# A new order of weight units in the odd layer, splits asked for earlier, and the norm's weights and bias applied by VectorE instead of GpSimd

## The reference

```python
h = layer_norm(x, g, b)                       # x: 256 x 1024
q, kv, gates, cq, ckv, k_rope = split_cols(h @ w_in, ODD_SPLITS)
cq, ckv = rms_norm(cq, g_q), rms_norm(ckv, g_kv)
# branch C: compressed, selected and window attention on q and kv
blocks = gelu(flat_blocks(kv_cmp + pe) @ w1) @ w2     # for keys and for values
# branch D: latent attention
q_d, k_d, v_d = cq @ w_uq, ckv @ w_uk, ckv @ w_uv     # with rotation of 32 of 96 channels
y = concat(attention_C, attention_D)
x = h * ALPHA + y @ w_out                     # then a layer norm and a conv feed-forward
```

## Time and profile before

| | |
|---|---|
| Median of 3 runs | 1433.69 us (1433.32 to 1433.8) |
| The profiled execution | 1439.07 us, of which the span of the profile is 1437.8 us |
| TensorE busy | 1322.6 us, 92% of the span |
| VectorE busy | 897.0 us, 62% |
| ScalarE busy | 590.5 us, 41% |
| GpSimd busy | 119.5 us, 8% |
| Mean granted clock of TensorE | 0.949 of full speed |

### The profile page before, as it was taken

How to read it: one execution, slowest core, us unless ns; L and a number is a source line. 1 busy time by engine, 2 the same in 40 slices (tenths; PEclk the granted TensorE clock), 3 DMA queues, 4 the chain that set the end, 5 groups by cost and what they waited for, 6 DMA issues and landing times. The chain is left out here.

```text
span 1437.8 us, 21155 instructions
## 1 busy us (share of the span) xinstructions
PE 1322.6 (92%) x8531; PEld 1204.6 (84%) x8537; DVE 897.0 (62%) x1291; ACT 590.5 (41%) x900; POOL 119.5 (8%) x152
## 2 busy tenths in 40 slices
PE   8988999999899999979987899999789898899996
PEld 5876788878589999869977799997779888799995
DVE  5957981125566777755476666666634585666666
ACT  2331111113355555543453554555411364554553
POOL 3890000003000000010000000010400000000000
PEclk9999899999999999999997999999887798999999
DMA  9434233427045556535502355565455202355561
GB/s 282 146 95 149 83 118 126 142 94 229 25 131 181 187 177 195 185 94 176 160 17 91 136 184 178 198 204 146 107 129 165 80 1 64 134 185 178 198 210 60
DMA packets 178590, 202.76 MB, mean 141 GB/s; under 512 B 21868, under 2 KB 163147, under 8 KB 178492
## 3 DMA queue, kind: packets, MB, share of 16 engines
q1 hardware_dynamic: 174939, 191.49, 42.0%
q0 software_dynamic: 3184, 9.77, 2.3%
q10 hardware_dynamic: 369, 0.13, 0.1%
HBM read 200.30 MB, written 1.08 MB: 140 GB/s over the span
## 5 line engine op out<-in xcount | busy, mean ns | idle before, releaser
L1317 DVE TENSOR_TENSOR w_parts<-raw,w_parts 128x1024 fp32r<-128x1024 f32 (+1 forms) x268 | 333.8, 1245 | 167.1 <-ACT w_parts L1306 159.6
L1306 ACT CAST w_parts<-raw 128x1024 fp32r<-128x1024 f32 (+1 forms) x268 | 279.3, 1042 | 337.6 <-PE ps L1600 103.3
L1600 PEld LDWEIGHTS ps<-hT_parts,w_parts 128*128 128x128 f32 x3024 | 366.6, 192 | 2.1
L1600 PE MATMUL ps<-hT_parts,w_parts 128*128 128x256 f32 x3024 | 367.6, 283 | 0.0
L1613 PE MATMUL ps<-w_parts,gT_parts 128*128 128x512 f32 x720 | 168.9, 390 | 0.0
L1613 PEld LDWEIGHTS ps<-w_parts,gT_parts 128*128 128x128 f32 x720 | 133.3, 188 | 26.4
L1366 PE MATMUL ps<-w_parts,hT_parts 128*128 128x256 f32 (+1 forms) x864 | 117.6, 303 | 16.7 <-DVE w_parts L1317 12.1
L1366 PEld LDWEIGHTS ps<-w_parts,hT_parts 128*128 128x128 f32 x864 | 116.2, 212 | 18.1 <-DVE w_parts L1317 12.5
L1364 PE MATMUL ps<-hT_parts,w_parts 128*128 128x256 f32 x912 | 120.8, 298 | 8.5 <-DVE w_parts L1317 4.5
L1364 PEld LDWEIGHTS ps<-hT_parts,w_parts 128*128 128x128 f32 x912 | 119.4, 207 | 10.0 <-issue 5.0
L451 PE MATMUL ps<-hT,ring 128*128 128x256 f32 x448 | 99.0, 380 | 1.0 <-DVE hT L310 1.0
(11 more groups left out here) (407 smaller groups left out, 1519.3 us busy)
## 6 DMA issues: line engine op xcount, KB each, us to landing
raw<-in_ffn_w_up SPq DMA_DIRECT2D x44, 1024.0 KB, 5.1
raw<-in_f_w_up SPq DMA_DIRECT2D x22, 1024.0 KB, 5.1
raw<-in_ffn_w_down SPq DMA_DIRECT2D x22, 1024.0 KB, 5.1
ring<-in_w_in SPq DMA_DIRECT2D x18, 1024.0 KB, 6.1
raw<-in_ev_w_in SPq DMA_DIRECT2D x15, 1024.0 KB, 5.4
raw<-in_f_w_down SPq DMA_DIRECT2D x11, 1024.0 KB, 4.9
ring<-in_x_wkv SPq DMA_DIRECT2D x8, 1024.0 KB, 5.5
ring<-in_w_out SPq DMA_DIRECT2D x4, 1024.0 KB, 5.1
```

The lines of the kernel that those rows point to most:

```text
L1306: self.done(A, A.copy(high[:, c], self.raw[:, u % RAW, c]), self.s_hi)
L1317: self.done(V, V.tensor_tensor(low[:, c], self.raw[:, u % RAW, c], high[:, c].bitcast(F32), ALU.subtract), self.s_lo)
L1600: mm = T.matmul(self.ps[:, b, m * 256:m * 256 + 256], w[:, kk, m * P:(m + 1) * P], x[:, kk, :], start=kk == 0 and q == 0, stop=kk == KD - ...
```

## The change

The list of units gets another order behind kv1. Before it is uq0, uq1, uk, uv, q0, cmp0, q1, cmp1, k0, cmp2, k1, cmp3. After it is q0, uq0, uq1, q1, uk, uv, k0, cmp0, cmp1, k1, cmp2, cmp3. TensorE follows this order. ScalarE and VectorE ask for the splits of q0, q1, k0 and k1 earlier in their queues, so ahead of some copies out of PSUM. GpSimd's `pool_affine` is gone. VectorE applies the weights and bias in eight pieces: two after the split of kv1, two after the split of k1, and four after the split of the first unit of `w_out`. GpSimd waits for these eight before it loads the next rows. No arithmetic is changed.

```diff
+        queries(0)
+        self.u_uq.append(unit(I["od_w_uq_2"][0], 0, 3, 512, False))
+        self.u_uq.append(unit(I["od_w_uq_2"][0], 512, 3, 256, False))
+        queries(1)
         self.u_uk, self.u_uv = unit(I["od_w_uk_2"][0], 0, 2, 512, False), unit(I["od_w_uv_2"][0], 0, 2, 512, False)
+        keys(0)
+        compress(0)
+        compress(1)
+        keys(1)
+        compress(2)
+        compress(3)
...
# TensorE
         ckf = self.pe_transposes(ckn, kt=2)
+        qf_ = self.pe_late(self.u_q[0], "F", self.hparts)
         self.pe_wait_drained(cqf)
         uqf = self.pe_late(self.u_uq[0], "T", cqT) + self.pe_late(self.u_uq[1], "T", cqT)
+        qf_ += self.pe_late(self.u_q[1], "F", self.hparts)
         self.pe_wait_drained(ckf)
         ukf = self.pe_late(self.u_uk, "T", ckT)
         uvf = self.pe_late(self.u_uv, "T", ckT)
+        kf_ = self.pe_late(self.u_k[0], "F", self.hparts)[0]
         T.wait_ge(*self.s_xs.at(8))
-        qf_, self.cmp_fills = [], []
-        qf_ += self.pe_late(self.u_q[0], "F", self.hparts)
+        self.cmp_fills = []
         self.pe_compress(0, 0, XS)
-        qf_ += self.pe_late(self.u_q[1], "F", self.hparts)
         self.pe_compress(0, 1, XS)
-        kf_ = self.pe_late(self.u_k[0], "F", self.hparts)[0]
+        vf_ = self.pe_late(self.u_k[1], "T", self.hparts)[0]
         self.pe_compress(1, 0, XS)
-        vf_ = self.pe_late(self.u_k[1], "T", self.hparts)[0]
         self.pe_compress(1, 1, XS)
...
# ScalarE
+        self.act_split(self.u_kv[1])
+        self.act_split(self.u_q[0])
         self.act_drain_gain(cqf, cqT, "od_q_norm_2", kt=3)
+        self.act_split(self.u_q[1])
+        self.act_split(self.u_k[0])
+        self.act_split(self.u_k[1])
         for hh in range(2):
             self.act_evac(uvf[hh], vm[:, :, hh * 256:(hh + 1) * 256])
+        self.act_split(self.u_odo[0])
+        for kv in range(2):
+            self.act_compressed(kv, hid)
...
# VectorE
+        self.dve_split(self.u_kv[1])
+        self.dve_affine(0)
+        self.dve_affine(1)
         V.wait_ge(*self.s_zero.at(2))
+        self.dve_blocks(0, kvf[0], KS, XS)
+        self.dve_split(self.u_q[0])
+        self.dve_blocks(1, kvf[1], KS, XS)
         self.dve_drain_gain(cqf, cqT, "od_q_norm_2", kt=3)
         self.dve_drain_gain(ckf, ckT, "od_kv_norm_2", kt=2)
+        self.dve_split(self.u_q[1])
+        self.dve_evac_halves(qf_[0], qT[:, :, 0:2, :])
         for hh in range(2):
             self.dve_evac(uqf[hh], uq[:, :, hh * 256:(hh + 1) * 256])
+        self.dve_split(self.u_k[0])
         self.dve_evac(uqf[2], uq[:, :, 512:768])
+        self.dve_rotate(0, uq, qf, kf)
+        self.dve_evac_halves(qf_[1], qT[:, :, 2:4, :])
         # copies of ukf, unchanged
+        self.dve_rotate(1, uq, qf, kf)
+        self.dve_split(self.u_k[1])
+        self.dve_affine(2)
+        self.dve_affine(3)
         self.dve_evac(kf_, kT)
+        self.dve_split(self.u_odo[0])
+        for i in range(4, 8):
+            self.dve_affine(i)
         self.dve_evac(vf_, vv)
...
# GpSimd
-        self.pool_affine(8)
...
+        if l == 1:
+            self.G.wait_ge(*self.s_affine_x.at(16))
```

More of the change, by code:

```diff
@@ L1227, in late_units @@
             self.u_kv.append(len(lu) - 1)
-        self.u_uq = [unit(I["od_w_uq_2"][0], 0, 3, 512, False), unit(I["od_w_uq_2"][0], 512, 3, 256, False)]
-        self.u_uk, self.u_uv = unit(I["od_w_uk_2"][0], 0, 2, 512, False), unit(I["od_w_uv_2"][0], 0, 2, 512, False)
[L1230 to L1244, removed]
+        self.u_q, self.u_k, self.u_uq, self.u_cmp = [], [], [], []
@@ new lines, in queries, with keys @@
+        def queries(i):
+            lu.append(((KD, 2, 2, 64), lambda v: [
+                (v[:, :, m, g, :], wk[:, :, g * 256 + (2 * i + m) * 64:g * 256 + (2 * i + m) * 64 + 64])
+                for m in range(2) for g in range(2)], 4, True))
+            self.u_q.append(len(lu) - 1)
+        def keys(i):
+            lu.append(((KD, 256), lambda v, c0=768 + 128 * i: [
+                (v[:, :, 128 * b:128 * b + 128], wk[:, :, c0 + 256 * b:c0 + 128 + 256 * b]) for b in range(2)], 2, True))
+            self.u_k.append(len(lu) - 1)
@@ new lines, in compress @@
+        def compress(i):
+            kv, half = divmod(i, 2)
+            w1 = I["od_cmp_w1_2"][0, kv].rearrange("(j p) n -> p j n", p=P)
+            lu.append(((8, 256), lambda v: [(v, w1[:, 8 * half:8 * half + 8, :])], 1, False))
+            self.u_cmp.append(len(lu) - 1)
+        queries(0)
+        self.u_uq.append(unit(I["od_w_uq_2"][0], 0, 3, 512, False))
+        self.u_uq.append(unit(I["od_w_uq_2"][0], 512, 3, 256, False))
+        queries(1)
+        self.u_uk, self.u_uv = unit(I["od_w_uk_2"][0], 0, 2, 512, False), unit(I["od_w_uv_2"][0], 0, 2, 512, False)
@@ L1549, in pool_rows @@
         self.G.dma_start(self.rowsb[:, i, 0:n], src.partition_broadcast(P)).then_inc(*self.s_rows[i].inc(16))
[L1551 to L1559, removed]
     def new_ffn(self, l, at):
@@ L2373, in layer_tail @@
         self.new_stats(2)
-        self.G.wait_ge(*self.s_affine_x.at(8 * l + 8))
+        self.G.wait_ge(*self.s_affine_x.at(16 * l + 8))
         for i in range(2):
@@ L2523, in odd_layer @@
             self.drain(V, V.tensor_copy(part(1), src(1)), f)
[L2524 to L2530, removed]
+        self.dve_rotate(1, uq, qf, kf)
+        self.dve_split(self.u_k[1])
+        self.dve_affine(2)
+        self.dve_affine(3)
         self.dve_evac(kf_, kT)
-        self.dve_split(self.u_cmp[2] + 1)
-        self.dve_split(self.u_k[1] + 1)
+        self.dve_split(self.u_odo[0])
+        for i in range(4, 8):
+            self.dve_affine(i)
         self.dve_evac(vf_, vv)
-        self.dve_split(self.u_cmp[3] + 1)
         V.wait_ge(*self.full(kcf))
@@ L2543, in odd_layer @@
         self.dve_parts(yf)
-        V.wait_ge(*self.s_affine.at(2))
         for c, u in enumerate(self.u_odo):
```

21 lines of the change are left out of this document (1 added, 20 removed).

## The result

The changed kernel takes 1421.16 us (median of 4, 1419.36 to 1422.45), where the kernel before takes 1433.74 (1433.32 to 1439.42). The ratio is 0.9889, with a 95% interval of 0.9863 to 0.9916. The medians differ by 12.6 us, and I had forecast 8.0.

The account below looks back on a forecast made before the run. TensorE, busy in 92% of the span, was taken to bound the kernel through its waits and clock. Moving cmp3's end from 1120.7 to 1112.8 gave 8.0 us off the 1433.7 median: 1425.7 us, range 1418.5 to 1431.

Parts of the forecast that it names:

- half clock of 2.5 us: In uv's second half and k0: TensorE's clock falls after uv's waits, costing 2.5 us.
- part 1: At od1 and od2: without GpSimd's four operations VectorE's split halves speed up, and od2 ends 6.8 us earlier.
- rival D: At od1 and od2: GpSimd and VectorE do not disturb each other, leaving 1.2 us gained, 1432.5 us; chance 0.07.
- parts 2 and 3: kv1 still waits, nothing gained; q0 fills the wait of 3.07 us before uq0, with VectorE's two pieces hidden behind kv1.
- q1's split in time: At q1: its weights are split at 1051.2, before TensorE needs them at 1057.0, so it runs at full clock.
- parts 5 and 6: From uv through k0: waits of 2.3 and 3.6 us at uv, then 2.5 us of half clock; k0 ends at 1084.1.
- part 6: Compression in pairs: the clock falls within each, 10.2 us a pair, k1 8.3, the second pair ending at 1112.8.
- the forecast 7.9: Over the odd layer's projections and compression: the end of cmp3 moves from 1120.7 to 1112.8, by 7.9 us.
- What follows (...) began at half clock before, and will again: Behind cmp3 (second layer of the compression, transposes, attention): starts at half clock as before, so no change was counted.
- B: More gained: k0's split in time (1417.3, or half, 1421), or clock kept through the pairs (1417.4); chance 0.17.
- C: Less gained: each pair's second block costs 7.3 us, and the clock falls again from uk to k0; 1429.6; chance 0.15.
- E: Slower: k0's weights land late and VectorE's early ask holds up uv; 12 us late gives 1437.7; chance 0.06.

Follow-up runs that it names:

- before_pieces: Kernel before, with GpSimd's four operations replaced by VectorE's eight pieces behind its last split of the odd layer's projections, unit order unchanged: 1425.46 us, ratio 0.9931.
- after_on_gpsimd: Changed kernel with the new order, but the norm's weights and bias back on GpSimd in four operations at their old place: 1426.39 us, ratio 0.9949.
- before_gpsimd_late: Kernel before, with GpSimd's four operations let go only when kv1 has been used: 1433.04 us, ratio 0.9987.
- after_no_pieces: Changed kernel with VectorE's eight pieces left out, so the odd layer's norm weights and bias are not applied: 1418.37 us, ratio 0.9887.
- after_zeros: Changed kernel with 16 matmuls of zeros, 512 columns each, among the records of cmp0 and cmp1 only: 1416.77 us, ratio 0.9869.
- after_drains_first: Changed kernel with VectorE copying out uq1, turning the first tile and copying out q1 before k0's split: 1416.46 us, ratio 0.9864.

## Why the prediction was right in kind and too small in size

The direction and, in the stretch, the mechanisms and their places were right. The size was not: 8.0 us forecast, 12.6 to 15.2 measured in three comparisons of medians. Two steps failed. The half clock of 2.5 us that I put behind uv's waits measured nothing (item 3). And I took everything outside the stretch as constant and left the new order, without part 1, 1.2 us; it measured 7.0, most of it outside the stretch (item 5).

1. **GpSimd and VectorE (part 1).** Right. od1 starts 4.1 us earlier against od0 and the clock stays up: from od0 to the end of od2 it is 26.5 us before and 19.9 after, so 6.7 less, where 6.8 was forecast. before_pieces has the same 19.9 and after_on_gpsimd the same 26.5. The rival D is out, by before_gpsimd_late above all: what counts is that both run at the same time.
2. **kv1 and q0 (parts 2 and 3).** Right to 0.2 us, as was q1's split in time. The first two pieces are hidden; after_no_pieces shows it.
3. **uv's wait and k0 (parts 5 and 6).** The place was right, the terms were mis-sized. I had waits of 2.3 and 3.6 and then 2.5 us for half clock in uv's second half and k0. There were 3.15 and 1.78, and the half clock fell in uv's first half instead, beside VectorE's rotation:

```profile
1064.00:1066.00 2.00, 2.00 (x6) 0.50 0.40 141
```

That half took 3.57 us, and it cost the path nothing: the second half had to wait for the copies anyway. uv's second half and k0 ran at full clock, 1.99 and 6.10. From the end of uk to the end of k0 it took 1076.3 - 1060.2 = 16.1 us, and I had 17.8.
4. **The pairs (part 6).** From start to start, the first pair took 9.6 us against 10.2 and k1 8.0 against 8.3; the second pair took 10.23. That is 0.9 us less together. The clock fell in both pairs, as forecast. That this comes from what the compression matmuls are, and not from a wait, is shown by after_zeros, and by after_drains_first, where it fell without the waits ahead. The few columns are the nearest reading, since the unsplit f32 matmuls of 256 columns kept the clock (uq0 and uq1, 36 records in 7.93 us); smaller steps between 30 and 256 columns were not run. By the Trainium skill, "TensorE: Matmul & The Clock Gate", section "HAM oscillation", waits let the clock fall. The first rows of after_zeros' section disagree if waits are taken as the only cause: the engine was busy in 2.00 of 2.00 us.
5. **The sum.** Items 3 and 4 account for the stretch: 1.7 and 0.9 us on top of the forecast 7.9 make the 10.4 of the first two profiles, within rounding. They do not account for the total, and the 7.9 was less well founded than it seemed. It started from one profile of the kernel before, with 117.2. In the second profile, of an execution close to the median (1433.46 us), the stretch was 114.1. Against that one the three profiles of the changed kernel gain 7.3 to 7.9 us in the stretch, close to the forecast by luck, and 11.1 to 15.8 in the span.

   The step that failed is "What follows (...) began at half clock before, and will again": I put everything outside the stretch at nothing. Behind it the profiles of the changed kernel took 317.0, 312.9 and 315.7 us, after_on_gpsimd 311.0, and those of the kernel before 317.1 twice. before_gpsimd_late, with the old order, has 317.0 too, while ten profiles of kernels with the new order and nothing edited behind cmp3 spread from 311.0 to 321.3, eight of them at 315.7 or less. That the granted clock makes this difference is in the rows.

   So behind the old order the same time came out in three profiles, and behind the new one it did not. The total gain is no luck, since the slowest execution of the changed kernel, 1422.45 us, is below the fastest of before, 1429.44. How much of it comes from behind the stretch, and what sets the clock there, stays open. So does the part ahead of od0, where the changed kernel was 2.8 to 6.2 us shorter in the profiles although nothing had changed there; that may be chance, since the kernels with edits further on spread over the same 995.4 to 1003.4. The one edit meant to fix the clock in the attention did not.

Of the rivals, B came nearest in size, for neither of its reasons: k0 was late, and the clock fell in both pairs. C and E did not happen.

## What to carry to other kernels

Look at what runs beside a slow instruction, on the engine that shares its memory interface, before you ask what it waits for. When a load is asked for early, count what is queued behind the asking: here two copies out of PSUM stood behind a split that waited for a transfer, and moving them ahead, together with a little filler work in matmuls of few columns, is worth another 9 to 12 us (1409.05 against 1418.13 to 1421.16). An edit to a kernel with many falls of the clock needs several profiled executions of both kernels before its size is believed, and a forecast that holds everything outside the edited stretch constant should say what that rests on.

## What the runs showed of the hardware

- VectorE and GpSimd take turns when both read two operands from SBUF. The split halves of 1024 and 736 elements take 2.97 to 3.31 us beside GpSimd and 1.22 and 0.93 without it, and additions of 120 elements up to 2.39 instead of 0.39. A copy out of PSUM beside the same operations took 0.69, as without them.
- TensorE at 100% busy fell from 1.00 to 0.50 of its clock in matmuls of 30 columns, in both pairs of the changed kernel. Sixteen matmuls of 512 columns of zeros among 64 records kept it at 1.00, and the pair with the unit behind it took 15.1 us instead of 17.6 (16.0 to 17.7 in all profiles without zeros), although they are extra work. Ahead of score matmuls in the attention, 16 such matmuls did not hold it: it fell 1.4 us into the groups.
- The same 48 matmuls of kv1 behind the same wait of 3.9 us took 8.71 us in one profile of the kernel before and 7.30 in another, and 7.29 to 8.67 behind that wait in the new order. Outside any change, the time up to od0 varied from 995.4 to 1003.5 us over the profiles of this study.
